# Weight blocks of whole rows beside the expert gathers, with the sums of a group kept in PSUM

## What is computed

```python
# first block
xn = rmsnorm(h, attn_norm)
q_a, k_a, v_a, q_r, k_r, v_r, g_r, gate_a, gate_r = split(xn @ w_in)
y_a = sliding_window_attention(q_a, k_a, v_a, sinks) @ w_attn_branch     # 1024 -> 2048
y_r = retention(q_r, k_r, v_r, g_r) @ w_ret_branch                       # 2048 -> 2048
h = h + (sigmoid(gate_a) * y_a + sigmoid(gate_r) * y_r) @ w_out
hn = rmsnorm(h, ffn_norm)
# peer: 8 heads, 16 of 16384 experts each, by products of two key sets
s = (hn @ w_query) against sub_keys; top 16 of 128, twice; top 16 of their 256 sums
act = gelu(hn . expert_down[idx])                  # 128 rows of 2048 for each token
h = h + sum(gate * act * expert_up[idx])           # 128 rows of 2048 for each token
x = rmsnorm(h, final_norm)
# second block
proj = rms_norm(x) @ w_in_2       # q, k, v, forget gate, rx, rg
h = x + concat(forgetting_attention, gated linear recurrence) @ w_out_2
h = h + hierarchical_moe(rms_norm(h))              # 32 experts, 2 for each token
out = h + sigmoid(rms_norm(h) @ w_ple_gate) * (p @ w_ple_up)
```

## Time and profile before

| | us |
|---|---|
| median of three runs | 3403.74 |
| the profiled execution | 3401.01 |
| its span, first to last instruction | 3399.2 |
| TensorE busy | 3131.6 (92%) |
| VectorE busy | 1086.3 (32%) |
| ScalarE busy | 572.8 (17%) |
| GpSimd busy | 649.7 (19%) |
| bytes moved | 1143.93 MB |

### The profile page before, as it was taken

How to read it: one execution, slowest core, us unless ns; L and a number is a source line. 1 busy time by engine, 2 the same in 40 slices (tenths; PEclk the granted TensorE clock), 3 DMA queues, 4 the chain that set the end, 5 groups by cost and what they waited for, 6 DMA issues and landing times.

```text
span 3399.2 us, 24836 instructions
## 1 busy us (share of the span) xinstructions
PE 3131.6 (92%) x8509; PEld 1379.7 (41%) x8509; DVE 1086.3 (32%) x1806; ACT 572.8 (17%) x1344; POOL 649.7 (19%) x598
## 2 busy tenths in 40 slices
PE   8999999998889999899798888898889989999999
PEld 4444444443333333334344333433344533333344
DVE  1030010024334334345364644533332132222220
ACT  1110010001211211112132312211122110001010
POOL 0000000003333333333343433333300000000000
PEclk9999999999999999999999999999999989999999
DMA  7534458869999999999999999999967749999982
GB/s 245 165 106 144 146 182 287 314 227 390 407 412 409 410 411 410 411 396 411 412 412 414 414 414 414 413 415 414 414 236 271 265 177 412 422 422 422 422 319 74
DMA packets 297701, 1143.93 MB, mean 337 GB/s; under 512 B 14416, under 2 KB 17024, under 8 KB 205696
## 3 DMA queue, kind: packets, MB, share of 16 engines
q1 hardware_dynamic: 223248, 605.17, 47.2%
q0 software_dynamic: 74352, 537.48, 38.5%
HBM read 1140.49 MB, written 2.10 MB: 336 GB/s over the span
## 4 chain that ended last, share of the span: by engine, by line
PE 56%; DMA 33%; DVE 4%; issue 3%; ACT 2%; DVEq 1%; SPq 0%; ACTq 0%; POOL 0%; POOLq 0%
PE bank L791 22%; DMA W<-in_peer_expert_down,big 15%; PE bank L782 12%; PE bank L1207 8%; DMA W<-in_w_expert_up 7%; DMA W<-in_w_in 4%; PE bank L1310 4%; PE bank L1365 3%; DMA W<-in_w_ret_branch 3%; DVE W L2121 2%; DMA W<-in_w_peer_query 2%; DMA W<-in_w_out 1%; PE bank L1294 1%; PE bank L1280 1%; PE bank L1334 1%
## 5 line engine op out<-in xcount | busy, mean ns | idle before, releaser
L2121 DVE CUSTOM_DVE_ANT_0 W<-W,big 128x2048 f32<-128x2048 f32 x256 | 585.7, 2292 | 731.8 <-DMA W<-in_peer_expert_down,big 731.0
L791 PE MATMUL bank<-W,XT 128*128 128x512 f32 x1408 | 634.7, 607 | 37.2 <-DMA W<-in_w_in 29.9
L1207 PE MATMUL bank<-XS,big 128*128 128x512 f32 x1040 | 488.4, 616 | 74.4 <-ACT big L1593 74.4
L719 POOL DMA_INDIRECT W<-in_peer_expert_down,big x256 | 290.9, 1136 | 1233.3 <-issue 697.5
L791 PEld LDWEIGHTS bank<-W,XT 128*128 128x128 f32 x1408 | 272.8, 195 | 381.9 <-issue 364.9
L782 PE MATMUL bank<-W,XT 128*128 128x512 f32 x960 | 417.5, 595 | 5.0 <-issue 5.0
L791 PE MATMUL bank<-W,big 128*128 128x512 f32 x896 | 398.6, 601 | 23.9 <-DMA W<-in_w_ret_branch 12.8
L1207 PEld LDWEIGHTS bank<-XS,big 128*128 128x128 f32 x1040 | 199.7, 197 | 341.2 <-issue 258.8
L1207 PE MATMUL bank<-W,big 128*128 128x512 f32 x520 | 248.0, 622 | 46.7 <-ACT big L1593 46.7
L782 PEld LDWEIGHTS bank<-W,XT 128*128 128x128 f32 x960 | 182.4, 191 | 227.5 <-issue 227.0
L791 PEld LDWEIGHTS bank<-W,big 128*128 128x128 f32 x896 | 171.6, 193 | 238.8 <-issue 224.6
(11 more groups left out here) (328 smaller groups left out, 1766.8 us busy)
## 6 DMA issues: line engine op xcount, KB each, us to landing
W<-in_w_in SPq DMA_DIRECT2D x102, 2048.0 KB, 8.4
W<-in_w_expert_gate SPq DMA_DIRECT2D x68, 1024.0 KB, 15.0
W<-in_w_expert_up SPq DMA_DIRECT2D x68, 1024.0 KB, 17.0
W<-in_w_out SPq DMA_DIRECT2D x32, 2048.0 KB, 9.3
big<-in_w_expert_down SPq DMA_DIRECT2D x32, 2048.0 KB, 12.6
W<-in_w_ret_branch SPq DMA_DIRECT2D x16, 2048.0 KB, 9.7
W<-in_w_peer_query SPq DMA_DIRECT2D x16, 2048.0 KB, 21.0
W<-in_w_attn_branch SPq DMA_DIRECT2D x8, 2048.0 KB, 8.5
```

The costliest lines, as they stand in the source:

```text
L719: pool.indirect_dma_start(down_row(n), None, down_t, row).then_inc(down_in[n % DOWN_ROWS], 16)
L791: mm = pe.matmul(out, lhs(k), slot(i)[:, k, :], start=first and k == 0, stop=last and k == 7)
L1207: mm = pe.matmul(bank[4 * (n // P) + c][:, :], DIAG[:, n % 4, :], up_row(n)[:, c * CH:(c + 1) * CH], start=n % P == 0, stop=n % P == P - 1)
L2121: dve.tensor_tensor_reduce(out=down_row(n), in0=down_row(n), in1=HN[n // P], scale=1.0, scalar=0.0, op0=ALU.mult, op1=ALU.add, accum_out=d ...
```

## The change

Three things change, all in the stretch beside the picks.

1. The 44 units of tile t = 1 of the first block (gate_a 8, gate_r 8, attention branch 4, retention branch 8, mix 8, query 8) become blocks of 256 rows by all 2048 columns: two pieces of 8 KB for each partition. The bytes are the same. One group (say, all of gate_a) now sums into banks 4 to 7 at once, all four column blocks together, and is complete only with its last unit. The units stand 2.15 ticks apart. Gates of t = 1 are kept in `P1[:, 1, VR..]` and `P1[:, 1, GR..]`; `weigh` multiplies the attention branch in, `merge_wide` the retention branch.
2. The 28 units of tile t = 0 of the second block (`in2` 20, `out2` 8) become blocks of 512 rows by 1024 columns: four pieces of 4 KB for each partition, into banks 0 and 1 together.
3. The tables follow: what took a column block out of its bank when that block was done now stands behind the group's last unit, four at a time. `FIFTH` goes from 104 to 109, the last query unit of t = 1 from tick 113 to 104.

The ring's slots, the gathers, the picks, the matmuls' number and size, and everything before tick 6 and behind the last pick are as before.

```diff
-    for t in range(T2):
-        gates = [...]
-        branch = [...]
...
+    for name in WIDE:
+        order += [(name, 1, j) for j in range(4 if name == "att" else 8)]
+    order += [("in2", 0, g, j) for g in range(5) for j in range(4)]
+    order += OUT2[0]
...
+WIDE = ("gate_a", "gate_r", "att", "ret", "mix", "query")
+OUT2 = [[("out2", 0, g, j) for g in range(2) for j in (2, 3, 0, 1)],
...
-        when[ORDER[i]] = int((i - first) * 2.42)
...
+    for name in WIDE:
+        units = [key for key in ORDER if key[:2] == (name, 1)]
+        for i, key in enumerate(units):
+            when[key] = int(at + i * 2.15)
+            put(pe, when[key], *key)
+        x = when[units[-1]]
+        at = max(at + len(units) * 2.15, x + 2)
+        for c in range(4):
+            if name in ("gate_a", "gate_r"):
+                put(act, x + 1, "gate", 1, WIDE.index(name), c)
+            elif name == "att":
+                put(dve, x + 1, "weigh", c)
+            elif name == "ret":
+                put(dve, x + 1, "merge", 1, c)
+                put(pe, x + 2, "turn_merged", 1, c)
+                put(act, x + 3, "turn_merged", 1, c)
+                at = x + 3
+            elif name == "mix":
+                put(dve, x + 1, "mix", 1, c)
+                put(pe, x + 2, "turn1", 1, c)
+                put(act, x + 2, "squares", 1, c)
+                put(dve, x + 3, "turn1", 1, c)
+                at = x + 3
...
+    fifth = x + 5
...
+                if t == 1 and kind in WIDE:
+                    return wide_from[kind].rearrange("(k p) n -> p k n", p=P)[:, 2 * key[2]:2 * key[2] + 2, :]
+                if t == 0 and kind == "in2":
+                    at = col[CHUNK_E[2 * key[2]][0]]
+                    return w2.rearrange("(k p) n -> p k n", p=P)[:, 4 * key[3]:4 * key[3] + 4, at:at + 1024]
...
+            def wide_unit(name, j):
+                ...
+                pe.wait_ge(w_loaded[SLOT[i]], LANDED[i])
+                if first and name in ("mix", "query"):
+                    for c in range(3):
+                        bank_free(name, c)
+                w = slot(i, D)
+                for c, k in [(c, k) for c in range(4) for k in range(2)] if first or last else [(c, k) for k in range(2) for c in range(4)]:
+                    if first and k == 0:
+                        bank_free(name, c)
+                    ...
+                    mm = pe.matmul(bank[4 + c][:, :], lhs, w[:, k, c * CH:(c + 1) * CH], start=first and k == 0, stop=last and k == 1)
+                    if last and k == 1 and c < 3:
+                        mm.then_inc(wide_chunk, 1)
+                mm.then_inc(w_used, 1)
...
+            def weigh(c):
+                dve.wait_ge(*wide_done("att", c))
+                dve.wait_ge(gate_kept, 8 + c + 1)
+                a = P1[:, 1, VR + c * CH:VR + (c + 1) * CH]
+                TT(a, a, bank[4 + c][:, :], ALU.mult).then_inc(weighed, 1)
+
+            def merge_wide(c):
+                dve.wait_ge(*wide_done("ret", c))
+                dve.wait_ge(gate_kept, 8 + 4 + c + 1)
+                a, r = (P1[:, 1, at + c * CH:at + (c + 1) * CH] for at in (VR, GR))
+                TT(r, r, bank[4 + c][:, :], ALU.mult)
+                dve.drain()
+                TT(a, a, r, ALU.add).then_inc(merged, 1)
```

More of the change, by code:

```diff
@@ L43, in order_of_units @@
     order = [("in", u) for u in range(30)]
-    for t in range(T2):
[L45 to L55, removed]
+    gates = [[("gate", 0, n, which, half) for which in range(2) for half in range(2)] for n in range(4)]
+    branch = [[("att", 0, n)] + [("ret", 0, n, half) for half in range(2)] for n in range(4)]
+    order += gates[0] + gates[1] + branch[0] + gates[2] + branch[1] + gates[3] + branch[2] + branch[3]
+    order += [("mix", 0, c, half) for c in range(4) for half in range(2)]
+    order += [("query", 0, c, half) for c in range(4) for half in range(2)]
+    for name in WIDE:
+        order += [(name, 1, j) for j in range(4 if name == "att" else 8)]
+    order += [("in2", 0, g, j) for g in range(5) for j in range(4)]
+    order += OUT2[0]
+    order += [("in2", 1, c, half) for c in range(10) for half in range(2)]
+    order += OUT2[1]
     return order + [("ple", j) for j in range(8)]
-OUT2 = [[("out2", 0, c, half) for c, half in ((0, 1), (1, 1), (0, 0), (1, 0), (2, 1), (3, 1), (2, 0), (3, 0))],
+WIDE = ("gate_a", "gate_r", "att", "ret", "mix", "query")
+OUT2 = [[("out2", 0, g, j) for g in range(2) for j in (2, 3, 0, 1)],
         [("out2", 1, c, half) for half in (1, 0) for c in range(4)]]
@@ L136, in steps_beside_picks @@
[L136 to L151, removed]
@@ L176, in steps_beside_picks @@
             put(pe, when[key], *key)
-        x = {c: when["in2", t, c, 1] for c in range(10)}
+        x = {c: when["in2", 1, c, 1] if t else when["in2", 0, c // 2, 3] for c in range(10)}
         put(pe, start + 1, "forget", t)
@@ new lines, in bank_free @@
+            def bank_free(name, c):
+                if name == "gate_a":
+                    if c < 2:
+                        pe.wait_ge(query_kept, 3 + c)
+                    else:
+                        pe.wait_ge(qt_kept if c == 2 else s_kept, 4)
+                elif name in ("gate_r", "att"):
+                    pe.wait_ge(gate_kept, 8 + 4 * (name == "att") + c + 1)
+                elif name == "ret":
+                    pe.wait_ge(weighed, c + 1)
+                elif name == "mix":
+                    pe.wait_ge(merged_kept, 4 + c + 1)
+                else:
+                    pe.wait_ge(kept1, 4 + c + 1)
@@ L877, in turn_query @@
-                turn_four(bank[6], QN[:, c % 2, :]).then_inc(query_turned, 1)
+                if t == 0 and c:
+                    pe.wait_ge(qt_kept, c)
+                elif t == 0:
+                    pe.wait_ge(kept1, 4)
+                turn_four(qt_out(t, c), QN[:, c % 2, :]).then_inc(query_turned, 1)
             def key_scores(t, c):
@@ L1105, in turn2, with paired_unit @@
                 turn_four(bank[c], H[:, t, c * CH:(c + 1) * CH]).then_inc(turned2, 1)
-            def in2_unit(t, c, half):
+            def paired_unit(key, lhs, first, last):
+                i = INDEX[key]
+                pe.wait_ge(w_loaded[SLOT[i]], LANDED[i])
+                for c in range(2):
+                    for k in range(4):
+                        mm = pe.matmul(bank[c][:, :], lhs(k), slot(i, 1024)[:, k, c * CH:(c + 1) * CH],
+                                       start=first and k == 0, stop=last and k == 3)
+                mm.then_inc(w_used, 1)
@@ L1537, in _ @@
                 for which in range(2):
-                    keep_gate(0, n, which)
+                    keep_gate(n, which)
             for j in range(4):
@@ L2127, in _ @@
                 for kind, *what in BESIDE_DVE.get(n, ()):
-                    if kind == "merge":
-                        merge(*what)
+                    if kind == "weigh":
+                        weigh(*what)
+                    elif kind == "merge":
+                        merge_wide(*what[1:])
                     elif kind == "mix":
```

348 lines of the change are left out of this document (195 added, 153 removed).

## The result

| | before | after |
|---|---|---|
| median of four runs, us | 3403.21 (3400.24 to 3407.13) | 3371.35 (3369.84 to 3375.01) |
| the profiled execution's span, us | 3399.2 | 3368.6 |
| mean granted clock of TensorE | 0.971 | 0.973 |

The ratio is 0.9906, with a 95% interval of [0.9894, 0.9919]: 31.9 us faster. The forecast was a gain of 20.0 us (3383.7); its own best end was 3374, and more than 30 us was rival 3.

What follows compares the result with a forecast made beforehand. The prediction took the DMA engines, always full, to bound the loop over the picks. Terms of -17.2, -6.0 and +3.2 us summed to -20.0, from a median of 3403.7 to 3383.7 us; the range went from 3374 to 3409.

Steps and rivals of the forecast that it cites:

- rival 3: Whole kernel: a gain of more than 30 us, only if the end of weight waits brought something by itself; chance 0.03.
- The bound: Loop over the picks: all 16 DMA engines always move packets, about 410 GB/s, so time follows bytes; TensorE comes second.
- Part 1: 44 units of t = 1, first block: pieces of 8 KB for 2 KB gain 17.2 us (12.2 to 17.9).
- Part 2: 28 units of t = 0, second block: pieces of 4 KB gain 6.0 us (nothing to 9.0).
- Part 3: Handovers in groups of four: four places cost 6.4 us, a hole that goes gives back 3.2; net +3.2 us.
- The old hole: In mix, VectorE stood 23.91 us behind a late unit, at 384 GB/s; it goes, -3.2 us.
- Turns between the queues: DMA engines alternate between queues: units land in 10 us with 8 KB, 15 with 4 KB; gathers take longer.
- Rival 1: Hardly any gain, 0 to 7 us: queues run dry at handovers, or pieces did not cause 390 against 422; chance 0.20.
- Rival 2: Part with the units: TensorE becomes the bound, 95.8% busy, deciding from 31 us of waits; 3414 us; chance 0.15.

Runs made afterwards that it cites:

- p2k: The changed kernel with its groups, ticks and bytes, but all 72 changed units in pieces of 2 KB, two DMAs of 1 MB each; 3400.72 us, ratio 0.9989.
- part1_only: The changed kernel with `in2` and `out2` of t = 0 put back as in the kernel before (2 KB pieces, one bank at a time); 3377.53 us, ratio 0.9922.
- pace16_fifth: The changed kernel with its t = 1 units 1.6 ticks apart, not 2.15, and the fifth selection begun at tick 96, not 86; 3370.05 us, ratio 0.9907.
- pace16: The changed kernel with its units of t = 1 placed 1.6 ticks apart in place of 2.15; 3384.36 us, ratio 0.9942.

## Why the prediction was wrong by 12 us, step by step

**The bound: right.** The DMA share is 1.01 in the dense part after as before, and the time follows the price of the bytes. The same bytes moved.

**Part 1, 17.2 us: mechanism right, term too small.** The price of 2 KB was taken as what is left of 400 us when the gathers have had theirs at 418 GB/s. The 418 came from the earlier trace rows, a stretch of 50 us with 622 packets between 512 B and 2 KB (949 less 327) that the gathers' own 8 KB pieces do not have. The changed kernel moves gathers and weights together at 421. With 421, 2 KB costs 2.597 us for 1 MB, 8 KB 2.378, and part 1 is 92.3 x 0.219 = 20.2 us, 3.0 more than forecast and above the upper end that I gave, 17.9. `p2k` against the changed kernel has 20.4 us at pick 128, with the 2.2 us of its two holes in them, and 29.4 - 6.2 = 23.2 in the medians, so some 18 to 21 without the holes: the term was too small, by 1 to 4 us.

**Part 2, 6.0 us: the argument right, the number partly luck.** Measured as 6.2 in the medians and as 7.3 to 7.8 between pick 128 and pick 255. The argument by pieces, two thirds of the way at half of the number of pieces, is borne out by three sizes: the step to 4 KB, 0.148, is 68% of the 0.219 to 8 KB. But the price of 2 KB was too low here as in part 1: the prices of this stretch give 58.7 x (2.594 - 2.458) = 8.0 us, and the deeper hole at 1850 took about 2 us back (2.9 us at 371 GB/s, 0.9 at the 399 of `part1_only`). The rule of the Trainium skill that the prediction weighed (page "DMA: Bandwidth & Descriptors", section "Why small descriptors are slow (HBM only)") would make both parts together 10.8 us; the runs show 26.4 (20.2 + 6.2). The rule's form, one price for each piece, agrees; its size, as the prediction worked it out, is too small here by more than a factor of two.

**Part 3, net +3.2 us: wrong, and of the wrong sign.** This is the step that failed. I priced a handover with 3.2 us, from the one row where VectorE stood 23.91 us. But in that row the unit was 7.69 us late, and in the same part I argued that units would be late no more: I took the lateness away and kept its price for the handover. With units in time VectorE waits 6.1, 3.5 and 2.8 us in all at the three groups, no slice of 10 us between 1000 and 1400 us falls below 416 GB/s, and the handovers cost nothing. The old hole did go, as said: 422 in place of 384. So the term is -3.2 and not +3.2.

`p2k` separates the two. At the same handovers VectorE waits up to 14.82 us for a late group, and the rate does not fall; its two holes stand at late units where VectorE waits for no group. The kernel before had shown this, and I had missed it: VectorE's waits of 16.11 us (to 1095 us) and 15.31 us (to 1340) stand in windows of 410 and 405 GB/s, and its other hole, 394 at 900 us, has no addition of VectorE near it, so the one at 1440 was not "the one such hole". What all four holes share is GpSimd, which stood 17.08 and 18.73 us (before, at 910 and 1453) and 17.67 and 17.86 us (`p2k`) without issuing a gather; its next longest stand, 16.20 us at 1170 in the kernel before, has a window of 404. That is read from four holes and was not tested by a kernel of its own. Whether VectorE's wait of 23.91 us made the hole at 1440 deeper than the others is open.

The sum with these terms is 20.2 + 6.2 + 3.2 = 29.6 us, against 30.6 in the profiled executions and 31.9 in the medians. The hole at 900 us, which went as well, is worth 25 x (1 - 394/410) = 1.0 more; the rest has no term. Working against the gain are the two dips behind the units of t = 1, 25 x (1 - 389/419) + 25 x (1 - 371/419) = 4.7 us, of which 1.0 was there before (397 of 414). Of the 11.9 us by which I missed the gain, part 3 has 6.4, part 1 by its price 3.0 and part 2 0.2 in the medians.

**Turns between the queues.** The direction was right, the sizes were not: 13.9 us for a unit of 8 KB pieces where I said 10, 18.5 for 4 KB where I said 15. What 8 KB takes from the gathers shows in their landing, 18.9 us where it was 12.9. With 4 KB, in the later stretch, the gathers land no later than before (15.3 against 15.7 us), where I had expected them to take longer.

**Rival 1, hardly any gain:** wrong. Queues do not run dry in the dense part, and 390 against 422 did come from the pieces. **Rival 2, TensorE as the bound:** wrong. TensorE is busy 663.7 of 720 us (92%), not the 95.8% that I worked out, and 377.7 of 400 (94%) in the dense part; even at over 95%, in `pace16_fifth` and in `pace16` up to 1400 us, the engines stay full. TensorE waits 56.3 us of the 720 and none of it for weights: with the queues full these waits are for gathered rows and diagonals, which is what a kernel bound by its bytes has. The condition "31 us of waits and the engines run dry" took every wait for a loss. **Rival 3, more than 30 us:** this came true, at a chance of 0.03. I had excluded it since full engines rule out a gain from shorter waits. That argument holds; what it left out was that the old hole goes without a price in its place, and that the price of the pieces itself was uncertain by 3 us on the good side. The range should have taken in that the handovers cost nothing at all together with part 1 at a gathers' rate of 421 or 422.

## What to carry to other kernels

When one change removes lateness and adds a handover, don't price the handover by a row in which something was late: look for rows that have the one without the other. Before a wait is given a price, look at the rate beside every other wait of its kind. Take the rate of a class of transfers from a stretch that holds nothing else, and look at the packet sizes in it, as 0.7% on the larger part of the bytes was 3 us on the smaller. And a loss that sits whole in one window of 25 us, as in `pace16`, calls for the chain of waits in that window before an engine is called full.

## What the hardware showed that I had not expected

A piece has a price of its own even at 2 to 8 KB. 1 MB costs 2.597, 2.449 and 2.378 us in 488, 244 and 122 pieces; 0.148 us for 244 pieces over 16 engines is, as an estimate, 16 x 0.148/244 = 9.7 ns of one DMA engine for each piece. By that estimate 1 MB in pieces of 8 KB still carries 0.07 us of it. Splitting one DMA into two, at the same size of pieces, costs nothing that can be told (3371.23 against 3371.35). With both queues full, the share that SyncE's queue gets grows with its pieces: its unit of 2 MB lands in 27.5 us with pieces of 2 KB, 18.5 with 4 KB and 13.9 with 8 KB, beside gathers of 8 KB (the 4 KB value is from the later stretch, where before a unit took 28.4).
